# Gathering each expert group's tokens by its own one-hot product, in a fused two-block transformer kernel

## The reference, cut to what matters

```
def one_seq(xs):                                  # xs: 256 x 1024, after layer norm "a"
    lg = (xs @ wr_g).astype(f32) + br_g           # 4 groups of experts
    pg = jax.nn.softmax(lg, axis=-1)
    ptop, gsel = lax.top_k(pg, 1)
    le = ((xs @ wr_e).astype(f32) + br_e).reshape(-1, MOE_GROUPS, MOE_PER_GROUP)
    le = jnp.take_along_axis(le, gsel[:, :, None], axis=1)[:, 0]
    lv, esel = lax.top_k(le, MOE_TOPK)            # two of the eight experts of that group
    we = jax.nn.softmax(lv, axis=-1) * ptop
    ...
    hg = jnp.einsum('sd,edh->seh', xs, w_gate)
    hu = jnp.einsum('sd,edh->seh', xs, w_up)
    h = jax.nn.silu(hg) * hu * gate[..., None].astype(xs.dtype)
    return jnp.einsum('seh,ehd->sd', h, w_down)
```

## Time and profile before

| | |
|---|---|
| median of three runs | 1759.92 us |
| profiled execution | 1755.09 us |
| its span | 1753.2 us |
| mean granted TensorE clock | 0.977 |
| TensorE busy | 1594.0 us (91%) |
| VectorE busy | 952.5 us (54%) |
| ScalarE busy | 728.2 us (42%) |
| GpSimd busy | 192.5 us (11%) |
| chain of waits | TensorE 74%, DMA 10%, VectorE 9% |
| DMA moved | 301.65 MB, mean 172 GB/s |

### The profile page before, as it was taken

How to read it: one execution, slowest core, us unless ns; L and a number is a source line. 1 busy time by engine, 2 the same in 40 slices (tenths; PEclk the granted TensorE clock), 3 DMA queues, 4 the chain that set the end, 5 groups by cost and what they waited for, 6 DMA issues and landing times.

```text
span 1753.2 us, 30856 instructions
## 1 busy us (share of the span) xinstructions
PE 1594.0 (91%) x11776; PEld 1228.4 (70%) x11776; DVE 952.5 (54%) x1701; ACT 728.2 (42%) x1326; POOL 192.5 (11%) x288
## 2 busy tenths in 40 slices
PE   7889889896866888999999999999999999989997
PEld 6776678894222235886675788888885877879997
DVE  5743564687512224275756555335535655578685
ACT  6332435643100125236745333323335655655455
POOL 0020011000100004003423000000013002220001
PEclk9989899997999999999999999999999999999999
DMA  6587724457999996320015422322235440256552
GB/s 248 190 214 270 253 97 133 144 181 278 364 409 409 409 405 195 101 95 25 2 57 192 146 89 83 108 96 96 73 109 205 141 135 13 85 197 188 181 192 73
DMA packets 84395, 301.65 MB, mean 172 GB/s; under 512 B 10080, under 2 KB 12128, under 8 KB 84128
## 3 DMA queue, kind: packets, MB, share of 16 engines
q1 hardware_dynamic: 80144, 288.92, 46.8%
q0 software_dynamic: 2736, 7.35, 1.8%
q10 hardware_dynamic: 1376, 3.47, 0.5%
HBM read 348.71 MB, written 3.15 MB: 201 GB/s over the span
## 4 chain that ended last, share of the span: by engine, by line
PE 74%; DMA 10%; DVE 9%; ACT 3%; issue 3%; SPq 1%; POOL 0%; ACTq 0%; DVEq 0%
PE bank L1041 53%; PE bank L997 14%; DMA ring<-wall 6%; DMA BIG<-wall 4%; PE bank L1623 3%; PE bank L1065 2%; DVE w_lo L2456 2%; ACT w_hi L1902 1%; PE bank L1659 1%; DMA lnst<-wall 1%; PE bank L1676 1%; SPq L866 1%; DVE SV L2504 1%; DVE BIG L2699 0%; DVE bank L2503 0%
## 5 line engine op out<-in xcount | busy, mean ns | idle before, releaser
L1041 PE MATMUL bank<-BIG_f32r,w_hi 128*128 128x256 f32 (+1 forms) x2208 | 546.0, 336 | 5.1 <-DVE w_lo L2456 2.9
L2456 DVE TENSOR_TENSOR w_lo<-ring,w_hi 128x1024 fp32r<-128x1024 f32 x261 | 322.1, 1244 | 285.7 <-ACT w_hi L1902 284.1
L1041 PEld LDWEIGHTS bank<-BIG_f32r,w_hi 128*128 128x128 f32 x2208 | 376.2, 189 | 61.2 <-issue 13.4
L1041 PE MATMUL bank<-BIG_f32r,w_lo 128*128 128x256 f32 (+1 forms) x1136 | 382.1, 336 | 0.0
L1902 ACT ACTIVATE w_hi<-ring 128x1024 fp32r<-128x1024 f32 x261 | 272.4, 1053 | 187.8 <-PE bank L1041 154.8
L1041 PE MATMUL bank<-AR_f32r,w_hi 128*128 128x256 f32 (+1 forms) x1050 | 271.6, 334 | 2.2 <-DVE w_lo L2456 2.2
L1041 PEld LDWEIGHTS bank<-BIG_f32r,w_lo 128*128 128x128 f32 x1136 | 214.5, 189 | 24.5 <-issue 0.7
L1041 PEld LDWEIGHTS bank<-AR_f32r,w_hi 128*128 128x128 f32 x1050 | 181.7, 189 | 25.7 <-issue 6.3
L1041 PE MATMUL bank<-AR_f32r,w_lo 128*128 128x256 f32 (+1 forms) x440 | 145.5, 331 | 0.0
L1041 PE MATMUL bank<-XC_f32r,w_lo 128*128 128x256 f32 x424 | 122.5, 289 | 0.0
L1041 PE MATMUL bank<-XC_f32r,w_hi 128*128 128x256 f32 x424 | 122.3, 288 | 0.0
(11 more groups left out here) (404 smaller groups left out, 2328.3 us busy)
## 6 DMA issues: line engine op xcount, KB each, us to landing
ring<-wall SPq DMA_DIRECT2D x423, 512.0 KB, 4.3
BIG<-wall SPq DMA_DIRECT2D x86, 512.0 KB, 15.3
w_extra<-wall ACTq DMA_DIRECT2D x11, 2048.0 KB
w_extra<-wall ACTq DMA_DIRECT2D x11, 1024.0 KB
AR<-wall ACTq DMA_DIRECT2D x5, 2048.0 KB
AR<-wall SPq DMA_DIRECT2D x16, 512.0 KB, 14.9
con<-wall SPq DMA_DIRECT2D x11, 512.0 KB, 12.4
BIG<-wall ACTq DMA_DIRECT2D x5, 1024.0 KB
```

Source lines behind the costliest of these rows:

```text
L1041: ins = nc.tensor.matmul(o, l, r, start=start and n == 0, stop=stop and n == 2, **kw)
L2456: V.tensor_tensor(w_lo[:, i % SPLIT_RING, :], ring[:, t % RING, :], w_hi[:, i % SPLIT_RING, :].bitcast(F32), ALU.subtract).then_inc(w_spli ...
```

## The change: what it does

1. **No sorted list.** `xt`, the turned X1, is kept as plain float32. For each group VectorE makes a one-hot matrix `m_hot` (256 tokens x 128 slots, function `hot`) and multiplies it by the gates into `m_sel` (`selection`). `moe_gather(g)` makes the group's tokens by 16 float32 matmuls (128 x 128, 128 columns) into banks 2 and 3, which are also the banks of `moe_down`; ScalarE copies bank 2 (`tokens_first`) and VectorE bank 3 (`tokens_last`) into `Xb`. GpSimd's copies, the 32 matmuls of `gx`, the splitting of `xt`, `sel` and `Xs` go.
2. **The order on TensorE.** `moe_gather(g + 1)` stands right behind `moe_up(g)`. `moe_down` also waits until banks 2 and 3 were copied.
3. **The overflow table** is made behind the first group's tokens, one block first and the other 15 in group 0's cycle.
4. **Far slots.** 20 instead of 18, so 26 slots. The first ten tiles go to arrays of the mixers that are no longer used; SyncE issues eight of them beside the last eight tiles of the merge and two beside the next ring tiles. The waits for `ln_out` and `gx` go: four tiles wait for the last `merged_split`, four stand behind `w_extra`, two wait for the bank of "var a".
5. **Constants** (128 columns instead of 512) are made in round 3 of the merge.
6. **Layer norms "a" and "f":** ScalarE writes six pieces of X1, VectorE the last two. Matmuls that nobody reads stand between the squares of "a" (one each) and ahead of `pos` (six of 256 columns).
7. The context is loaded after the first merge round, not the last.

The diff, cut; a line of `...` marks what is left out.

```
-FAR_ROUTED, FAR_LOW, FAR_SPARE, FAR_BIAS, FAR_TURNED = 4, 4, 4, 2, 4
-FAR = FAR_ROUTED + FAR_LOW + FAR_SPARE + FAR_BIAS + FAR_TURNED
+FAR_EARLY, FAR_SECOND, FAR_HALF, FAR_LOW, FAR_SUM = 10, 6, 4, 4, 2
+FAR = FAR_EARLY + FAR_HALF + FAR_LOW + FAR_SUM
+EARLY_BESIDE = 8
...
+            def early_expert_tile(j):
+                if j == 0:
+                    sp.wait_ge(sem("ys_split"), 4)
+                if j == FAR_STATS:
+                    sp.wait_ge(sem("merged"), 1)
+                assert slot_at[moe0 + j] == RING + j
+                sp.dma_start(far_tiles[j], expert_tile(moe0 + j)).then_inc(w_ready[RING + j], 16)
...
+                    if t == moe0 + FAR_EARLY + RING:
+                        sp.wait_ge(sem("merged_split"), KC)
+                    if t == moe0 + FAR_EARLY + RING + FAR_HALF:
+                        sp.wait_ge(w_used, last_split_use)
+                        for part, (q, n) in enumerate(((0, 4), (4, 2))):
+                            sp.dma_start(w_extra[:, q:q + n, :], wall[moe0 + q:moe0 + q + n].rearrange("k p c -> p k c"))\
+                                .then_inc(extra_ready[part], 16)
+                    if t == moe0 + RING + FAR - FAR_SUM:
+                        b, use = job[("var", "a")]
+                        sp.wait_ge(bank_ready[b], use)
...
+                    if moe0 - EARLY_BESIDE <= t < moe0:
+                        early_expert_tile(t - (moe0 - EARLY_BESIDE))
+                    if moe0 + FAR_EARLY <= t < moe0 + 2 * FAR_EARLY - EARLY_BESIDE:
+                        early_expert_tile(t - moe0 - FAR_EARLY + EARLY_BESIDE)
...
-            gp_.wait_ge(sem("merged"), KC)
+            gp_.wait_ge(sem("merged"), 1)
...
-            for g, blocks in enumerate(moe_of):
-                for j, b in enumerate(blocks):
-                    at = gp_.value_load(i_starts[0:1, b:b + 1], min_val=0, max_val=2 * S)
...
-                    nc.gpsimd.tensor_copy(Xb[:, g % 2, :, SLOTS * j:SLOTS * (j + 1)], Xs[:, :, bass.ds(at, SLOTS)])\
-                        .then_inc(sem("moe_x"), 1)
...
+                        if which == "a":
+                            mm(unread[:, 0:P], c_("ones"), c_("ident"))
...
+            idle_products(b, 6)
+            pe.wait_ge(sem("rt_chosen"), 2)
...
-            for k0 in range(0, KC, 4):
-                bs = [open_(("gx", k0 + k)) for k in range(4)]
...
+            def moe_gather(g):
+
+                pe.wait_ge(sem("moe_hot_sel"), 2 * g + 1)
+                if g >= 3:
+                    pe.wait_ge(sem("moe_y_low"), g - 2)
+                for k in range(KC):
+                    for t in range(2):
+                        ins = nc.tensor.matmul(ps[2 + k // 4][:, k % 4 * P:(k % 4 + 1) * P], xt[:, t, k * P:(k + 1) * P],
+                                               m_hot[:, g % 2, t, :], start=t == 0, stop=t == 1)
...
             def moe_down(g):
 
                 pe.wait_ge(sem("moe_hid"), g + 1)
+                pe.wait_ge(sem("moe_x_first"), min(g + 3, GROUPS))
+                pe.wait_ge(sem("moe_x_last"), min(g + 3, GROUPS))
...
+            moe_gather(0)
+            evacuated(pe, "pos")
             moe_select(0)
             for g in range(GROUPS + 2):
                 if g < GROUPS:
                     moe_up(g)
+                if g + 1 < GROUPS:
+                    moe_gather(g + 1)
                 if g >= 2:
                     moe_scatter(g - 2)
...
-                    for k in range(KC):
+                    for k in range(LN_ACT):
                         scaled(k)
...
+            def tokens_first(g):
+
+                act.wait_ge(sem("moe_gx"), 2 * g + 1)
+                f(Xb[:, g % 2, 0:4, :].rearrange("p k s -> p (k s)"), ps[2], ACT.Copy).then_inc(sem("moe_x_first"), 1)
...
+            def hot(g):
+
+                if g >= 2:
+                    dve.wait_ge(sem("moe_gx"), 2 * (g - 1))
+                own = sum(b < EXPERTS for b in moe_of[g])
+                b, extra, more_ = moe_of[g][0], moe_of[g][-1] - EXPERTS + 1 - (LANES - own), LANES - own
+                ins = V.tensor_tensor(at_lanes(m_hot, g, 0, own), each_slot(at_slot[:, :, b:b + own], own),
+                                      iota_away.unsqueeze(1).unsqueeze(1).broadcast_to([P, 2, own, SLOTS]), ALU.is_equal)
...
+            def tokens_last(g):
+
+                dve.wait_ge(sem("moe_gx"), 2 * g + 2)
+                V.tensor_copy(Xb[:, g % 2, 4:8, :].rearrange("p k s -> p (k s)"), ps[3]).then_inc(sem("moe_x_last"), 1)
...
+            step(V.scalar_tensor_tensor(at_slot, pos, AWAY + 1.0, rt[:, :, 1, :], ALU.add, ALU.mult))
+            hot(0)
...
+                if g + 1 < GROUPS:
+                    tokens_last(g + 1)
+                if g == 0:
+                    overflow_slots(1, EXTRA)
                 if g + 2 < GROUPS:
+                    hot(g + 2)
                     selection(g + 2)
```

More of the change, by code:

```diff
@@ L727, in build @@
         add(("mean", "a"), ("var", "a"), ("rs", "a"))
[L728 to L729 removed]
+        add("rt", ("xt", 0, 0), "lg", *[("xt", t, half) for t in range(2) for half in range(2)][1:], "pos")
         plan.append("MOE")
@@ new lines, in selection @@
+            def selection(g):
+                if g >= 2:
+                    dve.wait_ge(sem("moe_turned"), 2 * g - 3)
+                own = sum(b < EXPERTS for b in moe_of[g])
+                b, extra, more_ = moe_of[g][0], moe_of[g][-1] - EXPERTS + 1 - (LANES - own), LANES - own
+                ins = V.tensor_tensor(at_lanes(m_sel, g, 0, own), at_lanes(m_hot, g, 0, own),
+                                      each_slot(rt[:, :, 11, b:b + own], own), ALU.mult)
+                if more_:
+                    ins = V.tensor_tensor(at_lanes(m_sel, g, own, more_), at_lanes(m_hot, g, own, more_),
+                                          each_slot(slot_gate[:, :, extra:extra + more_], more_), ALU.mult)
+                tell(ins, "moe_hot_sel")
@@ L3003, in _ @@
-            at_slot = r_pos[:, 0, :, :]
-            frees(V.scalar_tensor_tensor(r_pos[:, 1, :, :], pos, AWAY + 1.0, rt[:, :, 1, :], ALU.add, ALU.mult), "pos")
-            evacuated(dve, "pos")
-            step(V.tensor_scalar(at_slot, r_pos[:, 1, :, :], AWAY, None, ALU.subtract))
-            step(V.tensor_scalar(more, cnt, float(SLOTS), None, ALU.is_gt))
-            for n in range(2, S // SLOTS):
-                step(V.scalar_tensor_tensor(more, cnt, float(n * SLOTS), more, ALU.is_gt, ALU.add))
@@ L3011, in _ @@
-            step(V.tensor_tensor_scan(more_upto, c_("scan_ones")[:, 0:32], more, 0.0, ALU.mult, ALU.add))
-            past, hot, prod = r_ov[:, 0, :, :], r_ov[:, 1, :, :], r_ov[:, 2, :, :]
-            nth_ = iota[:, 0:EXTRA]
-            whose, skipped, first_slot, round_, begin = [r_few[:, n, :] for n in range(5)]
-            step(V.tensor_tensor(past, bc(more_upto, EXTRA), over(nth_, 32), ALU.is_lt))
-            step(V.tensor_reduce(whose, past, AX.X, ALU.add))
-            step(V.tensor_tensor(prod, past, bc(more, EXTRA), ALU.mult))
@@ L3043, in _ @@
             step(ins)
[L3045 to L3057 removed]
+            selection(0)
@@ new lines, in _ @@
+            tokens_last(0)
+            past, whom, prod = r_ov[:, 0, :, :], r_ov[:, 1, :, :], r_ov[:, 2, :, :]
+            whose, skipped, round_, whose_1, capped = [r_few[:, n, :] for n in range(5)]
+            step(V.tensor_scalar(more, cnt, float(SLOTS), None, ALU.is_gt))
+            for n in range(2, S // SLOTS):
+                step(V.scalar_tensor_tensor(more, cnt, float(n * SLOTS), more, ALU.is_gt, ALU.add))
+            step(V.tensor_tensor_scan(more_upto, c_("scan_ones")[:, 0:32], more, 0.0, ALU.mult, ALU.add))
```

355 lines of the change are left out of this document (169 added, 186 removed).

## The result

The changed kernel takes 1738.87 us (median of 4 runs, 1737.98 to 1742.3), the kernel before beside it 1758.55. The ratio is 0.9904, 95% interval 0.9881 to 0.9926: about 17 us or 1% faster. Timed again later (median of 6 runs) it was 0.9913 (0.989 to 0.9937). The profiled execution took 1737.98 us, its span 1736.2. One execution of the later run gather_bf16 took 5050 us, for a reason that stays open, and stands in no median or ratio here.

What follows compares the result with a forecast made beforehand. Expert weight tiles arriving by DMA, not TensorE, were taken to bound the expert stage. 1755.09 - 17.0 (stage) - 0.8 (norm "f") = 1737.3 us profiled, plus 4.8 gives median 1742.1; range 1736 to 1753.

Steps and rivals of the forecast that it cites:

- The pipe's start: Expert stage: first used tile slots come free earlier, so the tile queue starts at about 425.5, 18.7 us earlier.
- the signs: Trace marks to confirm the forecast, among them first expert product at 420 to 423 us, last scatter at 648 to 650.
- Constants: Moved into the merge: norm input starts 0.8 us earlier; cost in the merge taken as 0, range 0 to 2.
- Norm "a": Six ScalarE pieces and clock-holding products: rows at 409.87 come 2.3 us earlier, constants' 0.8 included; range 0.8 to 3.
- Two slots: Expert stage's tile queue: 26 slots instead of 24 leave two tiles fewer behind the start, 2.6 us.
- What is late next: Expert cycles: gather hidden in waits up to group 6, TensorE the bound from group 8; stage end 17.0 us earlier.
- Norm "f": Last norm: six ScalarE pieces and VectorE's two end the chain 0.8 us earlier.
- The 4.8 us between the profiled execution and the median: Offset of the median above the profiled execution, added to 1737.3 to forecast a median of 1742.1 us.
- 1, the gather costs the cycle nothing: Expert stage: the tile pipe bounds to the end and hides the gather; median 1736.7 us; chance 0.10.
- 2, a gather of twice the length: Cycles of groups 7 to 11: unhidden weight loads, 7.7 us a gather, six counted; median 1763.4 us; chance 0.06.
- 3, the merge gives back: Merge slowed by early tile loads, or new hand-overs and VectorE work cost time; up to median 1752.1; chance 0.17.
- 4, no earlier start: An unseen wait holds the first gather; slots' 2.6 us are paid back by the cycles, no change; chance 0.05.

Runs made afterwards that it cites:

- gather_bf16: Changed kernel with the turned tokens kept as two bf16 parts and a bf16 0/1 matrix, so gathers use bf16 matmuls: 1734.09 us, ratio 0.9871.
- after_again: The changed kernel, unchanged, run and profiled a second time: ratio 0.9913 to the kernel before.
- gather_twice: Changed kernel with every gather issued twice into the same PSUM columns: 1755.85 us, ratio 1.0006.
- first_product_later: Changed kernel with twelve idle products of ones with a constant put ahead of gather 0: 1743.93 us, ratio 0.9933.

## Why the prediction was right

Predicted 1742.1 us, range 1736 to 1753; measured 1738.87. For the profiled execution 1737.3 against 1737.98. The mechanism held: an earlier start of the pipe, gathers hidden in the waits of the early groups, TensorE the bound in the last ones. That the numbers meet within 1 us is luck in part, since errors cancel in the stage and in the span. Step by step:

- **The pipe's start: right in its main part.** Forecast was 18.7 us earlier (425.5), with 8 us from the choice of experts to the first product. That piece measured 438.45 - 415.97 = 22.5 before and 418.55 - 410.66 = 7.9 after. The pipe started at 422.7, 21.5 us earlier; 2.0 of these are a merge that ended at 387.7 in that execution (384.6 to 392.7 in all of them). So the first product (418.55) and the last scatter (645.4) came earlier than the signs named (420 to 423, 648 to 650). One gather is 3.8 us where I took 3.9, gather 0 5.44 at a half clock that I had allowed for with 1.3 us.
- **Constants: mis-sized twice.** 0.8 gained and 0 paid in the merge; measured 2.9 (1.1 by the place, the rest by the width, as far as known) and 0.7 to 0.8. The three split tiles that I had between VectorE and TensorE don't hide it, since TensorE also waits for VectorE's low part of the merged tokens (0.51 us at 369.50). I read only the gap ahead of VectorE's first piece; the pieces also could not run beside the merge's last products, as they do at 385.61 now:

```profile
385.61 2.88 DVE L2986 SCALAR_TENSOR_TENSOR BIG<-XC,bank 128x256 f32<-128x256 f32 x8 [1.07 <-PE bank L1043]
```

- **Norm "a": failed as a step, hidden by the sum.** 2.3 us by the end of the choice, measured 3.3 from the end of the merge in after, 1.9 in after_again. Its parts are others: 2.9 by the constants, 1.7 by the mean's products at the full clock (3.72 instead of 5.41), 1.1 by the router's (3.85 instead of 4.93), against 2.7 for unread products between the squares, which I had counted as free.
- **Two slots: right in the queue, short in all.** 2.6, measured 2.5 by group 8 and 3.8 with the wait in group 11, which I had not.
- **What is late next: right in place, and in size by errors that cancel.** From the first expert product to the end of the stage I had 226.9 us and it is 226.85. The ends of the up products, from the first product on, for groups 6 to 11: predicted 120.5, 138.5, 156.4, 173.6, 190.8, 208.0; measured 121.0, 138.9, 158.3, 175.1, 192.0, 208.8. Group 8 ends 1.9 us later than I had it and still waits for a tile (2.6 us), though I wrote that TensorE is the bound from group 8 on. Then three cycles of 16.85 instead of 17.2 give 1.1 back, and the tail behind the last up product, 18.0 instead of 18.9, the rest: I had taken over from before a scatter at the half clock. The waits lie in groups 4 to 8 (4.7, 6.1, 6.2, 1.0, 2.6 us) and none in groups 0 to 3; my sum has waits in every cycle up to group 6.
- **Norm "f": failed.** 0.8 us expected, none came. From the reciprocal to the last piece it is 6.0 us instead of 7.0, but SyncE's eight issues start with the first piece and take 4.16 us before and 4.17 after. The last piece is ready 0.95 us earlier, but the queue of stores behind it is as late as before. Before and after:

```profile
1744.14 0.55 DVE L2569 RECIPROCAL lnst<-lnst 128x64 f32<-128x64 f32 x1 [0.41 <-ACT lnst L1993]
...
1747.31 4.16 SPq L871 DMA_DIRECT2D out<-XC  x8
```

```profile
1727.07 0.55 DVE L2601 RECIPROCAL lnst<-lnst 128x64 f32<-128x64 f32 x1 [0.41 <-ACT lnst L2017]
...
1730.24 4.17 SPq L884 DMA_DIRECT2D out<-XC  x8
...
1732.36 0.72 DVE L2636 TENSOR_SCALAR XC<-BIG,par 128x256 f32<-128x256 f32 x2
```

- **The 4.8 us between the profiled execution and the median: no constant.** It was 0.9 for the changed kernel. Its span is 0.8 us over the 1735.4 of my sum: 2.0 less ahead of the mark at the merge's end, 1.2 less to the first product, 4.0 more in the later stages, 0.8 of it norm "f". That these cancel is luck. Behind the last scatter after stood at the half clock for 22.7 us and before for 12.4, which fits the 3.2 that are left. And the median was forecast 3.2 us too high, for the 4.8.

**The rivals.** 1, the gather costs the cycle nothing: wrong, no wait for a tile in groups 9 to 11, and a quarter of the gather brings the cycle to 15.4. 2, a gather of twice the length: not so, and its price was near. In gather_twice, at 7.4 us with gather 0 at 9.01, the last scatter comes 280.1 us after the merge, 4.1 later than before's 275.9; my formula gives 2.5 for 7.4 us, and 4.3 for 7.7. The total is no slower than before (1.0006). Its formula, six gathers, is right only by balance: all twelve count, less 20.7 us of waits; near the kernel as it is, four do (gather 0 and those of groups 9 to 11). 3, the merge gives back: 0.7 to 0.8 us, by the constants and not by the transfers. VectorE's additional work on the way to group 2 costs a wait of 1.46 us. 4, no earlier start: wrong.

## What to carry to other kernels

- A pipe of prefetched tiles is timed by its first release. Time taken from ahead of that goes through one to one, and products moved into its waits are free until the waits are used up; count the tiles that are ahead, not only cycle against cycle.
- Products that keep the clock up are free only inside a wait. Between dependent pieces they are a stage of their own.
- Where the total moves by several us with the clock of stages that the change doesn't touch, cut both traces at the same marks and compare pieces, and take two profiles of the same kernel to see how far a piece repeats: this showed 0.76 us here, where the intervals of the timed runs were about 7 us wide or more.

## What the runs showed of the hardware

- The granted clock between the merge and the first expert product follows the work: two profiles of the kernel before agree on 0.79 there, ten of changed kernels with the idle products lie between 0.89 and 0.94, and the two without at 0.83 and 0.72. In long busy stages the pieces at the half clock come at other places in each execution; the stages behind the experts took 1083.5 us with 8.5 us at the half clock and 1091.0 with 26.2.
- TensorE busy in full for 82 us and the DMA at 409 GB/s hardly disturb each other: a gather at the full clock takes 3.73 us with the DMA at 0 GB/s (first_product_later, the first row) and 3.84 at 411 (after, the second).

```profile
422.73:426.46 3.73, 3.73 (x35) 3.71 (x33) 0.00 (x0) 1.73 (x2) 0.00 (x0) 1.00 0.00 0
```

```profile
471.94:475.78 3.84, 3.84 (x38) 3.84 (x35) 0.48 (x1) 0.98 (x2) 0.00 (x0) 1.00 1.03 411
```

- With one core running, the DMA holds 409 GB/s over 151 us. The Trainium skill (DMA: Bandwidth & Descriptors, Where 436 GB/s comes from) lets the HBM side bind loads from HBM at about 358 GB/s. No run here shows such a bound, and the measurement decides.
